# MLA and mLSTM trunk on one core: attention's value product in two passes of TensorE in place of three

## What is computed

```python
s = (einsum('bqhd,bkhd->bhqk', q_n, k_n) + einsum('bqhr,bkr->bhqk', q_r, k_r)) * scale
s = jnp.where(k_idx[None, :] <= q_idx[:, None], s, -jnp.inf)
p = jax.nn.softmax(s, axis=-1)
o = einsum('bhqk,bkhd->bqhd', p, v)
return o.reshape(B, S, 16 * 64) @ w_o
```

## Time and profile before

| what | value |
| --- | --- |
| median of 3 runs | 1216.26 us (1215.56 to 1216.5) |
| profiled execution: its own time | 1215.19 us |
| its span, first to last instruction | 1213.4 us |
| TensorE busy | 1196.4 us of the span (99%) |
| VectorE, ScalarE, GpSimd busy | 602.4, 453.8, 278.7 us |
| heads 0 to 15 of the attention | about 80 to 228 us of the span |

### The profile page before, as it was taken

How to read it: one execution, slowest core, us unless ns; L and a number is a source line. 1 busy time by engine, 2 the same in 40 slices (tenths; PEclk the granted TensorE clock), 3 DMA queues, 4 the chain that set the end, 5 groups by cost and what they waited for, 6 DMA issues and landing times.

```text
span 1213.4 us, 15687 instructions
## 1 busy us (share of the span) xinstructions
PE 1196.4 (99%) x6094; PEld 1011.2 (83%) x6094; DVE 602.4 (50%) x824; ACT 453.8 (37%) x726; POOL 278.7 (23%) x285
## 2 busy tenths in 40 slices
PE   7999999999999999999999999999999999999998
PEld 6778888888888888888879899988888888888887
DVE  6766666454334334344357645657443443433432
ACT  5467777433213222122334245544321221221234
POOL 2334234242002002012212135533210110210211
PEclk9999999999999999999999999999999999999999
DMA  6211112222332323322233434412233233332221
GB/s 188 53 36 29 25 36 94 80 89 85 105 104 90 97 91 104 104 83 91 73 103 105 148 92 97 117 35 92 82 105 104 71 103 104 104 104 81 92 74 71
DMA packets 117498, 107.43 MB, mean 89 GB/s; under 512 B 21334, under 2 KB 115764, under 8 KB 117436
## 3 DMA queue, kind: packets, MB, share of 16 engines
q1 hardware_dynamic: 117404, 106.56, 28.4%
q10 hardware_dynamic: 32, 0.01, 0.0%
HBM read 104.45 MB, written 2.11 MB: 88 GB/s over the span
## 4 chain that ended last, share of the span: by engine, by line
PE 81%; DVE 1%; issue 0%; ACT 0%; POOLq 0%; POOL 0%; DVEq 0%; ACTq 0%
PE ps L1590 25%; PE ps L1592 25%; PE ps L1591 25%; PE ps L2017 1%; PE ps L2019 1%; PE ps L2018 1%; PE ps L2046 1%; PE ps L2048 0%; PE ps L2047 0%; PE ps L1869 0%; PE ps L1871 0%; PE ps L1870 0%; PE ps L2029 0%; PE ps L1939 0%; PE ps L1616 0%
## 5 line engine op out<-in xcount | busy, mean ns | idle before, releaser
L741 ACT CAST whi<-raw 128x2048 fp32r<-128x2048 f32 (+3 forms) x149 | 184.9, 1271 | 265.2 <-PE ps L1592 254.7
L1124 DVE TENSOR_TENSOR wlo<-raw,whi 128x2048 fp32r<-128x2048 f32 (+3 forms) x90 | 197.6, 2198 | 151.3 <-ACT whi L741 151.2
L1590 PE MATMUL ps<-xl,whi 128*128 128x512 f32 (+1 forms) x624 | 245.1, 393 | 0.2 <-issue 0.2
L1591 PE MATMUL ps<-xh,whi 128*128 128x512 f32 (+1 forms) x624 | 243.0, 389 | 0.0
L1592 PE MATMUL ps<-xh,wlo 128*128 128x512 f32 (+1 forms) x624 | 242.9, 389 | 0.0
L1590 PE MATMUL ps<-ul,whi 128*128 128x512 f32 x576 | 224.7, 390 | 0.3 <-DVE wlo L1124 0.3
L1592 PE MATMUL ps<-uh,wlo 128*128 128x512 f32 x576 | 224.2, 389 | 0.0
L1591 PE MATMUL ps<-uh,whi 128*128 128x512 f32 x576 | 224.1, 389 | 0.0
L651 POOL TENSOR_TENSOR ul<-sq,uh 128x512 fp32r<-128x512 f32 x64 | 83.6, 1308 | 521.2 <-ACT uh L973 521.2
L1342 DVE TENSOR_TENSOR h<-ps,h 128x512 f32<-128x512 f32 x78 | 53.6, 689 | 181.5 <-PE ps L1592 178.0
L973 ACT CAST uh<-sq 128x512 fp32r<-128x512 f32 x64 | 39.7, 620 | 266.3 <-DVE sq L1374 266.3
(11 more groups left out here) (269 smaller groups left out, 1676.1 us busy)
## 6 DMA issues: line engine op xcount, KB each, us to landing
raw<-in_mlp_w SPq DMA_DIRECT2D x64, 1024.0 KB, 5.3
raw<-in_mlstm_w_in SPq DMA_DIRECT2D x12, 1024.0 KB, 5.3
raw<-in_mla_w_o SPq DMA_DIRECT2D x4, 1024.0 KB, 4.9
raw<-in_mlstm_w_o SPq DMA_DIRECT2D x4, 1024.0 KB, 5.3
raw<-in_mla_w_in SPq DMA_DIRECT2D x3, 1024.0 KB, 5.5
raw<-in_mla_w_uq SPq DMA_DIRECT2D x16, 192.0 KB, 2.5
x_tok<-in_x SPq DMA_DIRECT2D x4, 512.0 KB, 7.8
mx<-m_rows SPq DMA_DIRECT2D x8, 256.0 KB, 3.6
```

The costliest lines, as they stand in the source:

```text
L741: last = sc.copy(hi, src)
L1124: last = v.tensor_tensor(lo, src, hi.bitcast(F32), ALU.subtract)
L1590: mm(o, ah, bl, start=first, stop=False)
L1591: mm(o, ah, bh, start=False, stop=False)
```

## The change

The high and low values of one head stand side by side as one 128-column weight tile: `vhl` has, for each block of keys, four groups of 64 columns (even head high, even head low, odd head low, odd head high). `weigh` has two passes, that tile by `pth` and that tile by `ptl`. The bank then holds in 64 rows the part of the high values and in the other 64 the part of the low values; for an even head the high part is in rows 0 to 63, for an odd head in rows 64 to 127. The product low by low, which was left out before, is in it now. ScalarE copies the other half of the bank across (`o_second`) into `o_part`, VectorE adds bank and copy into `o_norm` (`o_add`), once per head; `o_scaled` then multiplies in place. `o_high` and `o_scaled` move from the start of an even head to its end. `weigh` of a head waits for the `o_add` of the head before.

```diff
--- before.py
+++ after.py
@@ -183,8 +183,8 @@
         cql = A("cql", [P, 4, S], F32R)
         ckvh = A("ckvh", [P, 2, S], F32R)
         ckvl = A("ckvl", [P, 2, S], F32R)
-        vh = A("vh", [P, TT, 3 * VD], F32R)
-        vl = A("vl", [P, TT, 3 * VD], F32R)
+        vhl = A("vhl", [P, TT, 4 * VD], F32R)
+        o_part = A("o_part", [P, S])
         prob = A("prob", [P, P * TT * (TT + 1) // 2])
         cos = A("cos", [P, S])
         sin = A("sin", [P, S])
@@ -216,13 +216,10 @@
 
             return v_all[:, i, :].rearrange("p (t e n) -> p t e n", t=TT, e=2)
 
-        def heads_of(t):
-
-            return t[:, :, :].rearrange("p t (r n) -> p t r n", r=3)[:, :, 0::2, :]
-
-        def gap_of(t):
-
-            return t[:, :, VD:2 * VD]
+        def v_parts(low):
+
+            quarters = vhl[:, :, :].rearrange("p t (r n) -> p t r n", r=4)
+            return quarters[:, :, 1:3, :] if low else quarters[:, :, 0::3, :]
 
         def prob_of(b):
 
@@ -341,6 +338,7 @@
         v_hi, v_lo = sem("v_hi"), sem("v_lo")
         s_mm, s_max, s_exp = sem("s_mm"), sem("s_max"), sem("s_exp")
         t_mm, t_hi, t_lo = sem("t_mm"), sem("t_hi"), sem("t_lo")
+        o_moved, o_sum = sem("o_moved"), sem("o_sum")
         w_mm, o_new, o_hi, o_lo = sem("w_mm"), sem("o_new"), sem("o_hi"), sem("o_lo")
         r_inv, rt_mm, rt_ready, r_mm, r_ready, pick_ready = (sem("r_inv"), sem("rt_mm"), sem("rt_ready"), sem("r_mm"),
                                                              sem("r_ready"), sem("pick_ready"))
@@ -585,8 +583,6 @@
             g.tensor_copy(onesr[:], ones[:, 0:2])
             g.tensor_copy(identr[:], ident[:])
             g.tensor_copy(maskr[:], mask_s[:]).then_inc(consts, 1)
-            for t in (vh, vl):
-                g.memset(gap_of(t).bitcast(F32), 0.0)
 
             def norm_adds(norm, end=False):
 
@@ -625,7 +621,7 @@
             def v_low(i):
 
                 pool.wait_ge(v_hi, i + 1)
-                g.tensor_tensor(heads_of(vl), v_slot(i), heads_of(vh).bitcast(F32), ALU.subtract).then_inc(v_lo, 1)
+                g.tensor_tensor(v_parts(True), v_slot(i), v_parts(False).bitcast(F32), ALU.subtract).then_inc(v_lo, 1)
 
             def o_low(i):
 
@@ -838,7 +834,15 @@
 
                 if i:
                     act.wait_ge(w_mm, 2 * i)
-                sc.copy(heads_of(vh), v_slot(i)).then_inc(v_hi, 1)
+                sc.copy(v_parts(False), v_slot(i)).then_inc(v_hi, 1)
+
+            def o_second(head):
+
+                e = head % 2
+                act.wait_ge(w_mm, head + 1)
+                if head >= 2:
+                    act.wait_ge(o_sum, head - 1)
+                sc.copy(o_part[64 * e:64 * e + 64, :], ps[64 - 64 * e:128 - 64 * e, B_PV, :]).then_inc(o_moved, 1)
 
             def o_high(i):
 
@@ -891,13 +895,13 @@
                 nxt = head + 1 < HEADS
                 if not second:
                     v_high(i)
-                    if i:
-                        o_high(i - 1)
                 elif nxt:
                     for e in range(2):
                         k_high(e, i + 1)
                 pt_high(head, 0)
                 pt_high(head, 1)
+                if head:
+                    o_second(head - 1)
                 if head + 3 < HEADS:
                     split(N_PAIR + head + 3, "q" if not second else "kq")
                 elif head + 3 == HEADS:
@@ -915,6 +919,8 @@
                 if nxt:
                     exp(head + 1, 2)
                     exp(head + 1, 3)
+                if i and not second:
+                    o_high(i - 1)
                 if second:
                     rows_spread(i)
                 if head + 2 == HEADS:
@@ -922,6 +928,7 @@
 
             for head in range(HEADS):
                 attention(head)
+            o_second(HEADS - 1)
             o_high(PAIRS - 1)
 
             def residual_stage(n0, t0, norm, gain):
@@ -1286,13 +1293,19 @@
                 own.link(v.tensor_copy(rinv2[:, 0:8], rinv[:]))
                 low(rinv2[:, 8:16], rinv[:], rinv2[:, 0:8]).then_inc(r_inv, 1)
 
+            def o_add(head):
+
+                i, rows = head // 2, slice(64 * (head % 2), 64 * (head % 2) + 64)
+                dve.wait_ge(o_moved, head + 1)
+                if head % 2 == 0 and i >= 2:
+                    dve.wait_ge(o_lo, i - 1)
+                v.tensor_tensor(o_norm(i)[rows, :], ps[rows, B_PV, :], o_part[rows, :], ALU.add).then_inc(o_sum, 1)
+
             def o_scaled(i):
 
-                dve.wait_ge(w_mm, 2 * i + 2)
+                dve.wait_ge(o_sum, 2 * i + 2)
                 dve.wait_ge(r_ready, i + 1)
-                if i >= 2:
-                    dve.wait_ge(o_lo, i - 1)
-                v.tensor_tensor(o_norm(i), bank(B_PV), r_b[:], ALU.mult).then_inc(o_new, 1)
+                v.tensor_tensor(o_norm(i), o_norm(i), r_b[:], ALU.mult).then_inc(o_new, 1)
 
             for e in range(2):
                 k_low(e, 0)
@@ -1308,8 +1321,6 @@
                 i, second = head // 2, head % 2
                 if second:
                     row_scales(i)
-                elif i:
-                    o_scaled(i - 1)
                 if second and nxt:
                     for e in range(2):
                         k_low(e, i + 1)
@@ -1317,6 +1328,8 @@
                 pt_low(head, 1)
                 if head + 2 < HEADS:
                     q_table(head + 2)
+                if head:
+                    o_add(head - 1)
                 if nxt:
                     row_max(head + 1, 0)
                 pt_low(head, 2)
@@ -1328,9 +1341,12 @@
                     row_max(head + 1, 3)
                 if head + 2 < HEADS:
                     q_low(head + 2)
+                if i and not second:
+                    o_scaled(i - 1)
 
             for head in range(HEADS):
                 attention(head)
+            o_add(HEADS - 1)
             o_scaled(PAIRS - 1)
             dve.wait_ge(o_lo, PAIRS - 1)
             dve.wait_ge(o_hi, PAIRS)
@@ -1744,20 +1760,17 @@
             def weigh(head):
 
                 e = head % 2
-                cols = slice(VD * e, VD * e + P)
+                cols = slice(P * e, P * e + P)
                 pe.wait_ge(t_hi, 4 * head + 4)
-                pe.wait_ge(v_hi, head // 2 + 1)
-                if e == 0 and head:
-                    pe.wait_ge(o_new, head // 2)
+                pe.wait_ge(v_lo, head // 2 + 1)
+                if head:
+                    pe.wait_ge(o_sum, head)
                 for j in range(TT):
-                    mm(ps[:, B_PV, P * j:S], vh[:, j, cols], pth[e][:, j, P * j:S], start=(e + j == 0), stop=False)
-                pe.wait_ge(v_lo, head // 2 + 1)
-                for j in range(TT):
-                    mm(ps[:, B_PV, P * j:S], vl[:, j, cols], pth[e][:, j, P * j:S], start=False, stop=False)
+                    mm(ps[:, B_PV, P * j:S], vhl[:, j, cols], pth[e][:, j, P * j:S], start=(j == 0), stop=False)
                 pe.wait_ge(t_lo, 4 * head + 4)
                 for j in range(TT):
-                    last = mm(ps[:, B_PV, P * j:S], vh[:, j, cols], ptl[e][:, j, P * j:S], start=False,
-                              stop=(e == 1 and j == TT - 1))
+                    last = mm(ps[:, B_PV, P * j:S], vhl[:, j, cols], ptl[e][:, j, P * j:S], start=False,
+                              stop=(j == TT - 1))
                 last.then_inc(w_mm, 1)
 
             def turn_scales(i):
```

## The result

The changed kernel takes 1235.88 us (median of 5 runs, 1235.73 to 1238.34) against 1215.78 (5 runs, 1215.31 to 1216.5) before: 20.1 us more, a ratio of 1.0169 with a 95% interval of 1.0158 to 1.0181. The forecast was 1232, in a range of 1222 to 1240. The profiled execution is the slowest of the five, 1238.34 us, 2.5 above the median; its span is 1236.5.

A forecast was written before the change was run, and what follows sets the result against it. TensorE was taken to bound the attention. Passes -10.2, waits +20.3, end +1.0, shifts in heads 13 to 15 +0.3 and clock +4.3 gave +15.7 on 1215.2, 1230.9; the median 1.1 above, 1232.0, range 1222 to 1240.

The forecast's parts named there:

- The saved passes: `weigh` on TensorE: one pass less in each of 16 heads at 0.64 us, 10.2 us less.
- The queue behind the moved step: GpSimd, even heads 2 to 12: strip stuck behind `o_low`, which awaits late `o_high`; six TensorE waits of 3.4 us, 20.3 more.
- The chain worked out: Head 8, `q_low` through `o_scaled`, `o_high`, `o_low` and strip: TensorE released at 165.94, against 162.56 without the wait.
- The clock: TensorE around the six waits: granted clock falls at three of six, 1.4 us each, 4.3 us more, between 0 and 10.8.
- a spell that begins 2 us into the wait: Price of one clock fall on TensorE if its first 1.4 us are idle: about 1.1 us.
- 3.6 us of slow work: Kernel start: transposes of 430 ns from 7.7 us, 272 by 12.2; taken as the length of a slow spell.
- VectorE's addition: `o_add` in each head, 0.69 us: pushes next `row_max` 0 by some 0.5, nearly all absorbed by 0.42 idle; no cost.
- The end of the attention: Before out-product 7: copy, add, scale, round, subtract take 3.65 us, so TensorE waits 1.0 us once (0.6 to 1.3).
- the 0.9 us wait of the earlier trace: TensorE, heads 13 to 15: shifts there put at 0.3 us, between -0.8 with that wait gone and 1.5.
- the rival near the old time: The six TensorE waits at half the length, the clock holding: 1216.4 us; chance 0.05.
- ScalarE as the bound: Rival: ScalarE's thin cover in the heads is spent, up to 9 us on the likeliest, 1241; chance 0.05.
- that GpSimd's strip would not be late: Faster rival, at `o_low` before `strip_low` in even heads: with no wait at all 1207.4 us; chance 0.08.

The follow-up runs named there:

- e4_swap_third: e1_swap with the first pass of the value product done twice, the first result overwritten: 1218.33 us.
- e3_fill: The changed kernel with twelve matmuls, their result overwritten, before TensorE's wait for the strip in heads 3, 5 ... 13: 1229.22 us.
- e1_swap: The changed kernel with GpSimd's order in even heads turned round, the strip's subtraction ahead of the attention output's: 1208.61 us.
- e8_early: The changed kernel, GpSimd's order kept, with `o_scaled` and `o_high` back in the middle of the even head: 1214.05 us.
- e2_before_swap: The kernel before the change, with only GpSimd's order in even heads turned round, strip ahead of `o_low`: 1215.53 us.
- e5_swap_late: e1_swap with VectorE's `o_add` three instructions later, behind `row_max` 1 of the next head: 1208.11 us.
- e6_double_add: e1_swap with VectorE's addition done twice in each head, the first into an unused tile: 1216.54 us.
- e7_double_copy: e1_swap with ScalarE's copy of half the bank done twice in each head, the first into an unused tile: 1210.44 us.

## Why the prediction was right, and where it was off

**The saved passes: right.** 10.2 us was forecast; e4_swap_third prices the pass at 9.7 us for 16, 0.63 to 0.65 a head up to head 13, and odd heads shrank by 0.63, from 8.85 to 8.22. The trace's 0.64 was the number to use, not the 0.54 from the Trainium skill (TensorE: Matmul & The Clock Gate, Back-to-back issue gap), whose formula is given there for isolated matmuls, while here each matmul has a weight load of its own (6030 of both on the page of the profile): the runs bear the trace out.

**The queue behind the moved step: right, in place, count and size.** Forecast: six waits, 3.4 us each, 20.3 in all, before the query products in the odd heads. Measured: six of 3.1 us idle in the waits' view, 3.36 each by the heads' length in e3_fill, 20.6 us in all. The chain worked out placed TensorE's release 12.25 us into head 8; it came at 12.44 (176.86 less 164.42), 0.2 late because `q_low` was (7.61 us into the head, where the text has 7.33). That the wait comes from `o_low`'s place in front of the strip was an argument before the runs; e1_swap and e8_early show it, each mending one end of the link, and e2_before_swap shows that the order alone costs nothing.

**The clock: right in kind, mis-sized.** Forecast: three falls of six at 1.4 us, 4.3 us. The profiled execution has five, and in two of them the lower level lasted about twice as long: the distances to heads 5 to 13 are 13.11, 14.38, 12.91, 13.10 and 14.36 us against 11.58, for the last 11.95, in e3_fill, so 1.5, 2.8, 1.3, 1.5 and 2.4 us, 9.5 in all. The median run lost less: 6.7 us, by e3_fill. So the price of one fall was well met for three of the five (1.3 to 1.5 us); the count and the two long ones were not, and this term is the largest of what the forecast missed: 6.7 against 4.3. The 1.1 us for a spell that begins 2 us into the wait was met by none; the earliest began in the last 0.7 us of its wait, two others 1.3 us behind it. The text took its 3.6 us of slow work from the start of the kernel, where only the lengths of transposes speak for it (the granted clock reads 1.00 in that stretch); the low stretches behind the second and fourth waits, 3.2 us and a little more, bear the size out.

**VectorE's addition: wrong.** The text said that `o_add`, pushing `row_max` 0 by 0.5 us, is taken up nearly all by 0.42 us of idle time. But that idle time stands behind `row_max` 0, in front of `row_max` 2, and helps only what comes after it. `row_max` 0 itself feeds `exp` 0, which frees the scores bank that TensorE's block 3 waits for, and on that branch a part only of the 0.6 us was covered. It cost 0.32 us in each of six even heads, some 2 us where nothing was in the sum; e5_swap_late takes it away, and e6_double_add shows that a further 0.60 there is paid nearly in full by even and odd heads alike (0.63 and 0.55).

**The end of the attention: right.** 1.0 us was forecast, 0.8 measured; the 0.9 us wait of the earlier trace rows fell to 0.2 in the changed kernel, in the bounds given (it is 0.7 in e1_swap, where nothing delays TensorE earlier).

**The sum.** By the medians: e1_swap 7.0 us below before (the passes at -9.7, the rest added work and the end), +20.6 for the waits, +6.7 for the clock: +20.3, against 20.1 measured. These are differences along one row of kernels, so that they add up proves nothing; what is shown is the size of each. Forecast for the same three were -8.9, +20.3 and +4.3, together 15.7. So the change was forecast 4.4 us too small, through `o_add` and the clock above all, and the median 3.9 too low: the 1216.3 taken for the kernel before was 0.5 above its later median, which was luck. A slip without effect: for the rival near the old time the text takes 9 us for waits of half the length; half of 20.3 is 10.2. Of the rivals, ScalarE as the bound falls with e7_double_copy; that GpSimd's strip would not be late gave 1207.4, and with the lateness taken away the kernel is at 1208.6.

## What to carry to other kernels

When a step is moved later, look at what stands behind its consumer on the consumer's own queue, not only at who wants its result: here nobody was in a hurry for `o_low`, but a weight strip stood behind it. A busy share of 22% tells nothing of that; GpSimd was the least busy of the four that compute, and in six heads it set the time. Exchanging two calls turned 1235.9 us into 1208.6. And price an idle stretch of TensorE with the slow matmuls behind it: here they cost 6.7 us on 20.6 of waiting.

## What the runs showed of the hardware that was not expected

The granted clock can fall after the gap, when matmuls run again: 1.3 us behind the wait in two of five cases, with TensorE busy in all of these 1.3 us, and then stay low for more than 3 us of full work, at the third wait for 6.6. The Trainium skill (TensorE: Matmul & The Clock Gate, Part 1) has an idle array throttled and released by activity; the direction agrees at five of the six waits, and in e3_fill above all, where twelve matmuls in each wait, whose result nobody reads, made the kernel 6.7 us faster. Why the first of six equal waits left the clock alone is open, and so is why two of the low spells were twice as long. How much is lost differs between executions: the five runs of the changed kernel have mean clocks from 0.990 to 0.993, and the profiled one has the lowest. Where the clock fell in the other four is not recorded.
